# Multiply-adds of the modulation in chosen quanta, their sums turned later, two small steps of the attention on ScalarE

## The reference, cut to what matters

```python
for l in range(2):
    mod = silu(c) @ w_mod[l] + b_mod[l]          # 3 * 2048 columns: shift, scale, gate
    cmod = silu(c_ctx) @ w_mod[l] + b_mod[l]
    h = rmsnorm(x, norm_g[l]) * (1 + scale) + shift
    u = h @ w_in[l]                              # heads' q, k, v and the columns of ug
    y = concat(mixer_1(u), mixer_2(u)) * silu(ug)
    x = x + gate * (y @ w_o[l])
# layer 0: mixers a and b, layer 1: mixers c and d. One head of b: softmax(q k^T + mask, sink) v.
# One head of a: (softmax(q1 k1^T) - lam * softmax(q2 k2^T)) v, then its own rmsnorm.
```

## Time and profile before

| what | value |
|---|---|
| three timed runs | 2482.7 (median), 2484.22, 2478.44 us |
| the profiled execution | 2480.8 us |
| its span, first to last instruction | 2479.0 us |
| TensorE matmuls, busy | 2384.4 us, 96% |
| TensorE weight loads, busy | 1917.5 us, 77% |
| VectorE busy | 1526.8 us, 62% |
| ScalarE busy | 1034.1 us, 42% |
| mean granted TensorE clock | 0.994 |

### The profile page before, as it was taken

How to read it: one execution, slowest core, us unless ns; L and a number is a source line. 1 busy time by engine, 2 the same in 40 slices (tenths; PEclk the granted TensorE clock), 3 DMA queues, 4 the chain that set the end, 5 groups by cost and what they waited for, 6 DMA issues and landing times. The chain is left out here.

```text
span 2479.0 us, 31391 instructions
## 1 busy us (share of the span) xinstructions
PE 2384.4 (96%) x11660; PEld 1917.5 (77%) x11660; DVE 1526.8 (62%) x2575; ACT 1034.1 (42%) x1712; POOL 233.1 (9%) x329
## 2 busy tenths in 40 slices
PE   6999999999899999999899999999999999999998
PEld 1587778877668878887777788878878888898886
DVE  1368766777677777757646566676576544444654
ACT  3322333344443222433444445445454545654543
POOL 0001010011100000002121000001110001101100
PEclk8999999999999999999999999999999999999999
DMA  9957544444334565565464465756655576567653
GB/s 367 355 188 259 169 159 137 149 144 153 112 122 137 189 202 178 189 217 196 165 216 137 129 209 176 248 174 192 211 159 191 180 219 207 174 198 239 182 194 127
DMA packets 231174, 467.96 MB, mean 189 GB/s; under 512 B 17642, under 2 KB 42536, under 8 KB 229744
## 3 DMA queue, kind: packets, MB, share of 16 engines
q1 hardware_dynamic: 209104, 394.94, 49.2%
q0 software_dynamic: 21920, 71.01, 9.0%
HBM read 435.10 MB, written 30.79 MB: 188 GB/s over the span
## 5 line engine op out<-in xcount | busy, mean ns | idle before, releaser
L2112 PE MATMUL pp<-w_hi,hT_hi 128*128 128x512 f32 (+3 forms) x2904 | 1169.9, 403 | 9.1 <-DVE w_lo L1512 3.9
L2114 PE MATMUL pp<-w_hi,hT_lo 128*128 128x512 f32 (+3 forms) x2904 | 1115.8, 384 | 0.0
L2113 PE MATMUL pp<-w_lo,hT_hi 128*128 128x512 f32 (+3 forms) x2904 | 1113.4, 383 | 0.0
L1512 DVE TENSOR_TENSOR w_lo<-raw,w_hi 128x1024 fp32r<-128x1024 f32 (+4 forms) x568 | 669.4, 1183 | 572.2 <-ACT w_hi L1234 570.8
L1234 ACT ACTIVATE w_hi<-raw 128x1024 fp32r<-128x1024 f32 (+4 forms) x568 | 578.0, 1023 | 436.7 <-PE pp L2114 383.3
L2112 PEld LDWEIGHTS pp<-w_hi,hT_hi 128*128 128x128 f32 x2904 | 547.3, 188 | 137.4 <-issue 35.3
L2114 PEld LDWEIGHTS pp<-w_hi,hT_lo 128*128 128x128 f32 x2904 | 546.1, 188 | 105.7
L2113 PEld LDWEIGHTS pp<-w_lo,hT_hi 128*128 128x128 f32 x2904 | 548.0, 189 | 94.7 <-issue 6.9
L1612 DVE SCALAR_TENSOR_TENSOR arena<-raw,cT,arena 128x512 f32<-128x512 f32 x240 | 172.3, 745 | 0.7
L1612 DVE SCALAR_TENSOR_TENSOR xy<-raw,cT,xy 128x512 f32<-128x512 f32 x180 | 126.8, 744 | 0.0
L1393 ACT ACTIVATE arena<-pY 128x512 f32<-128x512 f32 (+2 forms) x114 | 62.1, 544 | 138.5 <-PE pY L2273 106.0
(11 more groups left out here) (311 smaller groups left out, 1764.5 us busy)
## 6 DMA issues: line engine op xcount, KB each, us to landing
raw<-in_w_in_dram SPq DMA_DIRECT2D x168, 512.0 KB, 4.1
raw<-in_w_mod_dram SPq DMA_DIRECT2D x158, 512.0 KB, 5.0
raw<-in_e_w_in_dram SPq DMA_DIRECT2D x102, 512.0 KB, 4.8
raw<-in_w_o_dram SPq DMA_DIRECT2D x64, 512.0 KB, 4.6
raw<-in_o_w_in_dram SPq DMA_DIRECT2D x64, 512.0 KB, 4.8
raw<-in_w_out_dram SPq DMA_DIRECT2D x64, 512.0 KB, 4.0
raw<-in_w_in_dram SPq DMA_DIRECT2D x56, 440.0 KB, 3.9
scratch_u<-ust POOLq DMA_DIRECT2D x35, 512.0 KB, 4.4
```

The lines of the kernel that those rows point to most:

```text
L1512: dve.tensor_tensor(w_lo[:, g.s % SPLIT, 0:n], raw_of(g)[:, 0:n], w_hi[:, g.s % SPLIT, 0:n].bitcast(F32), ALU.subtract).then_inc(lo_done, 1)
L2112: pe.matmul(dst, hT_hi[:, kk, o:o + P], hi[:, k, :], start=a, stop=False)
L2113: pe.matmul(dst, hT_hi[:, kk, o:o + P], lo[:, k, :], start=False, stop=False)
L2114: ins = pe.matmul(dst, hT_lo[:, kk, o:o + P], hi[:, k, :], start=False, stop=z)
```

## The change

Four things. (1) `Work.room` gives for each quantum how many multiply-adds it may hold, in place of the rates: 1 and 2 in turn up to quantum 164, 1 for twelve quanta, then 1 in each even quantum among the heads of b, three in eight among those of a (places 3, 4 and 7 counted from 308), 5 in four quanta from y0_3 to c_q0, and from there two in four. `LEAD` is 3. (2) Two more accumulators, of which one lies where mixer a's raw q and k were and waits for its last front, and the other in half of b_mask for the chunks gate1 that have one lane; the seven quanta between chunks are gone where the accumulator is another one. Load 0 of mixer c waits for the fold of shift1_3. (3) A fold comes at least four quanta after the last multiply-add. (4) The copies of mixer b (32) and the divisions `finish` of mixer a (32) are ScalarE's.

```diff
-LEAD = 4
+LEAD = 3
+    def room(self, slot):
+        b0, a0 = C["a_q0"].q0 + 4, C["a_q0"].q0 + 148
+        if slot < b0:
+            return 1 + slot % 2
+        if slot < b0 + 12:
+            return 1
+        if slot < a0:
+            return (slot - b0) % 4 in (0, 2)
+        if slot < C["y0_3"].q0:
+            return (slot - a0) % 8 in (3, 4, 7)
+        if slot < C["c_q0"].q0:
+            return 1 + (slot % 4 == 2)
+        return (slot - C["c_kv"].q1) % 4 in (0, 1)
...
-        rate = [(C["b_q1"].q0 + 4, 1.0), (C["b_kv"].q0, 1.4), (C["a_q0"].q0 + 14, 0.65), (C["y0_0"].q0 + 24, 0.55), (C["y0_3"].q0, 1.0), (C["c_q0"].q0, 0.5)]
-        free_b, taken_a = C["a_q0"].q0 + 152, C["y0_0"].q0 + 20
+        free_b, free_c, taken_a, taken_c = C["a_q0"].q0 + 152, C["y0_0"].q0 + 92, C["y0_0"].q0 + 20, C["c_q0"].q0 + 40
...
+            late = ch.name.startswith("gate1")
+            ch.lanes = (0,) if late else (0, 1)
+            if late:
+                slot, used = max(slot, self.sides[i - 1].macs_end + (9 if self.sides[i - 1].row is None else 1)), 0
+            elif i and slot + 4 > taken_a:
+                same = [p for p in self.sides[max(0, i - 2):i] if p.acc == (3 if i % 2 == 0 and slot > free_c else 2)]
+                if same and same[-1].macs_end + 9 > slot:
+                    slot, used = same[-1].macs_end + 9, 0
...
+                    while used >= self.room(slot):
+                        slot, used = slot + 1, 0
+                    used += 1
                     g.macs.append(slot)
...
-            first, second = [s for s in free if s >= ch.macs_end + 2][:2]
-            assert ch.acc < 2 or second < ch.macs_end + 7
+            first, second = [s for s in free if s >= ch.macs_end + 4][:2]
+            assert second < ch.macs_end + 8
...
-        accs = [xy[:, 0:2, 512:1024], xy[:, 2:4, 512:1024], b_mask]
+        accs = [xy[:, 0:2, 512:1024], xy[:, 2:4, 512:1024], b_mask, at(5632, 2, 512), at(8704, 1, 512)]
...
+                if m == "c" and n == 0:
+                    pool.wait_ge(*folded(C["shift1_3"]))
...
             def copy(m, n, u):
-                if m == "b":
+                copies(act_copy, act, m, n, u)
+
+            def finish(m, n, u):
+                if m != "a":
                     return
-                copies(act_copy, act, m, n, u)
+                x = plan.U[m, n, u]
+                act.wait_ge(probed, prob_n[x.key])
+                act.wait_ge(filled["O"], left["O", ("pv", *x.key)])
+                c0 = MIX["a"].ycol + 128 * n
+                act.activation(xy[:, x.qt, c0:c0 + 128], pO[:, 0:128], ACT.Copy, scale=rl[:, x.i % 4, 0:1]).then_inc(freed["O"], 1)
...
+                    elif ch.acc == 3:
+                        for key in (("front_q", "a", 7), ("front_k", "a", 7)):
+                            dve.wait_ge(filled[bank_of[key]], left[bank_of[key], key])
+                    elif ch.acc == 4:
+                        dve.wait_ge(*folded(C["shift1_3"]))
...
-            def copy(m, n, u):
-                if m == "b":
-                    copies(dve_copy, dve, m, n, u)
-
             def finish(m, n, u):
+                if m == "a":
+                    return
```

More of the change, by code:

```diff
@@ L185, in run @@
             self.put(ch, j)
-    def rate(self, table, slot):
-        return [r for s, r in table if s <= slot][-1]
+    def room(self, slot):
+        C = self.C
+        b0, a0 = C["a_q0"].q0 + 4, C["a_q0"].q0 + 148
[10 more added lines that the diff above has]
+        return (slot - C["c_kv"].q1) % 4 in (0, 1)
     def beside(self):
         C = self.C
-        rate = [(C["b_q1"].q0 + 4, 1.0), (C["b_kv"].q0, 1.4), (C["a_q0"].q0 + 14, 0.65), (C["y0_0"].q0 + 24, 0.55), (C["y0_3"].q0, 1.0), (C["c_q0"].q0, 0.5)]
-        free_b, taken_a = C["a_q0"].q0 + 152, C["y0_0"].q0 + 20
+        free_b, free_c, taken_a, taken_c = C["a_q0"].q0 + 152, C["y0_0"].q0 + 92, C["y0_0"].q0 + 20, C["c_q0"].q0 + 40
         self.macs = []
-        slot, credit = rate[0][0], 0.0
+        slot, used = C["b_q1"].q0 + 4, 0
         for i, ch in enumerate(self.sides):
-            lanes = (0,) if ch.name.startswith("gate1") else (0, 1)
-            ch.lanes = lanes
-            ch.mac0 = slot
+            late = ch.name.startswith("gate1")
[6 more added lines that the diff above has]
+                    slot, used = same[-1].macs_end + 9, 0
             for j in range(KT_ // GROUP):
@@ L205, in beside @@
                 self.sided.append(g)
[L206 to L209, removed]
+                for K, v in itertools.product(g.ks, ch.lanes):
+                    while used >= self.room(slot):
+                        slot, used = slot + 1, 0
+                    used += 1
                     g.macs.append(slot)
                     self.macs.append((slot, ch, K, v))
[L212 to L215, removed]
                 g.q0 = g.macs[0]
[L217 to L221, removed]
+            ch.mac0, ch.macs_end = ch.groups[0].macs[0], g.macs[-1]
+            if late:
+                ch.acc = 2 + 2 * (i % 2)
+            elif ch.macs_end + 9 < taken_a:
+                ch.acc = i % 2
+            elif i % 2 == 0 and ch.mac0 > free_c and ch.macs_end + 9 < taken_c:
+                ch.acc = 3
+            else:
+                ch.acc = 2
+                assert ch.mac0 > free_b
         n = 0
@@ L1491, in _ @@
             mine = {"evac": evac, "fold_row": fold_row, "sq_x": sq_x, "x_scale": x_scale, "sq": sq, "sq_x2": sq_x2, "x_turn": x_turn, "y_turn": y_turn, "lat_turn": lat_turn,
-                    "front_copy": front_copy, "exp": exp, "copy": copy, "squares": squares, "kpe_turn": kpe_turn,
+                    "front_copy": front_copy, "exp": exp, "copy": copy, "finish": finish, "squares": squares, "kpe_turn": kpe_turn,
                     "i_turn": i_turn, "ik_turn": ik_turn, "i_dots": i_dots, "g_soft": g_soft, "g_exp": g_exp,
@@ L2018, in _ @@
                     "lat_turn": lat_turn, "x2": x2, "n2_scale": n2_scale, "n3_half": n3_half, "x_gain": x_gain, "x_out": x_out, "front_copy": front_copy,
-                    "ssq": ssq, "rope": rope, "max": max_, "probs": probs, "copy": copy, "finish": finish, "a_scale": a_scale,
+                    "ssq": ssq, "rope": rope, "max": max_, "probs": probs, "finish": finish, "a_scale": a_scale,
                     "kpe_rope": kpe_rope, "kpe_turn": kpe_turn, "i_rope": i_rope, "ik_rope": ik_rope, "i_acc": i_acc_, "i_top": i_top,
```

## The result

The changed kernel takes 2486.95 us in the median of 8 runs (2483.42 to 2489.48), the kernel before 2481.45 beside it. The ratio is 1.0021, 95% interval 1.0012 to 1.0029: 5 us slower. 2476.9 was forecast, 6 us faster, with slower at 0.19: the median lies within the range that was given (2467 to 2489), but on the other side of the kernel before. The profiled execution took 2483.42 us, its span is 2481.4 (before: 2480.8 and 2479.0).

What follows compares the result with a forecast made beforehand. TensorE was taken to lead, busy 96%, with waits on other engines mostly in mixer a. Terms -10.8 - 1.5 + 0.5 + 2.0 + 4.0 = -5.8 us gave a median of 2476.9 from 2482.7; range 2467 to 2489.

Steps and rivals of the forecast that it cites:

- Mixer a, -10.8: Mixer a: 10.8 us gained from finishes on ScalarE, new places and later folds; bounds 6 and 16.1.
- 2.6 + 4.1 + 2.8: Heads of a, finishes on ScalarE: shorter probability waits 2.6, waits behind squares gone 4.1, sum-transpose waits gone 2.8 us.
- a gain of 1.3: Mixer a, places and folds: gains of 1.4, 0.5 and 0.6 us, less 1.2 for a fold pair that comes in.
- Copies of b, 0: Mixer b: its 32 copies moved to ScalarE gain nothing; value 0, bounds -1 us and +3.
- b_q1 and b_kv, +0.5: b_q1 and b_kv: rate up to 1.5 a quantum, VectorE 74% to 89%; costs 0.5 us, bounds 0 and 3.
- y0_3, +2.0: y0_3: 39 multiply-adds for 32, VectorE 83% to 91%, slightly late when y is turned; costs 2 us (0 to 5).
- Mixer c, -1.5: Mixer c: multiply-adds end at quantum 676 where they ended at 723; gain 1.5 us, bounds 0 and 3.
- out0, +4.0 (bounds 1 to 14): out0 chunks: rate 1.25, 150 multiply-adds for 107, VectorE 74% to 90%; costs 4.0 us, bounds 1 and 14.
- four prices of VectorE's own work: out0: chunk ends 2.1 us, a fold that comes 0.8, one that goes -0.8, two more multiply-adds into c 1.0.
- The 0.9: out0: weight loads held up by the reload of x, buffers with 5 quanta for 8; 0.9 us, between 0 and 4.1.
- The slower one: y0_3 to c: VectorE becomes the bound when late weights use up the slack; 17 us lost there, 2487.9, chance 19%.
- The mark that I had set for being wrong: Sign against the forecast: TensorE's idle time above 15 us between 775 and 1023 us, among three such signs.

Runs made afterwards that it cites:

- e1: Kernel before with only the copies of b and finishes of a moved to ScalarE; places, folds, accumulators and LEAD as before: ratio 0.9957.
- e2: Changed kernel with the copies of b and finishes of a back on VectorE; places, folds, accumulators and LEAD as changed: ratio 1.0050.
- e5: Changed kernel with all but the first multiply-add of six sums on 256 of 512 columns; instructions, order and loads stay: ratio 0.9977.
- e9: Changed kernel with LEAD 2 in place of 3: ratio 0.9965.
- e6: Changed kernel with 35 multiply-adds per 32 quanta of out0 for 40, none around the turn into c, c at quanta 2 and 3 of four: ratio 0.9957.
- e4: Changed kernel with mixer c's multiply-adds at quanta 2 and 3 of each four in place of 0 and 1: ratio 1.0015.
- e11: e6 with LEAD 2: ratio 0.9958 to the kernel before.
- e14: e12 with LEAD 2: ratio 0.9942 to the kernel before.
- e15: e14 without second multiply-adds in y0_3's last twelve quanta and out0_0's first four; three go to out0_3: ratio 0.9932.
- e12: e6 with folds two quanta apart from y0_3 on, and gate1's multiply-adds one a quantum in c_kv, none in c_q1: ratio 0.9941.
- e13: e1 with LEAD 2 in place of 4: ratio 0.9960 to the kernel before.

## Why the prediction was wrong, point by point

**Mixer a, -10.8: near in size, and that partly by luck.** The heads of a gave 12.7 us. The finishes on ScalarE were put at 9.5 (2.6 + 4.1 + 2.8) and give 6.7 (e1, profiled); waits behind the squares and behind finishes went as said, save one of 1.0, but the waits for the probabilities, which were to shrink by 2.6, stayed: 7.6 us in 12 waits for 7.3 in 10. Places and folds were put at a gain of 1.3 and give 6.0 in the heads alone (e2); a term too large and one too small made up for each other. The waits for L1912 in the changed kernel are at most 1.4 us where they were up to 1.8, and the new one behind a fold (1.2 us at quantum 363, 1.2 forecast) is as sized. Two others of 1.4 stand at quanta 387 and 419. The Trainium skill's rule of "ScalarE: Activation LUTs", section "Rules for kernel authors", to leave multiplications to VectorE, would have made this part worth nothing; e1 measures 10.7 us for the two moves, so here the place in the queue decided, not the price of the instruction.

**Copies of b, 0: right** (+0.3 in e1). What was not expected is that b's heads gain 3.0 us by the new places (e2; 85 multiply-adds there for 110), where I had written that no wait was there. The earlier trace rows show 4.7 us idle in that stretch, and I had put it at nothing. **b_q1 and b_kv, +0.5:** 0.0 with LEAD 3 at 87% of VectorE. **y0_3, +2.0:** +0.3. **Mixer c, -1.5:** +2.1; behind quantum 676, where no multiply-adds are left, d_kv gained 2.9 us, and c_kv and c_q1, which have about as many as before (24 for 22), lost 6.2.

**out0, +4.0 (bounds 1 to 14): the step that failed.** It measures +17.9, above the upper bound. I summed four prices of VectorE's own work at places that I knew and gave the weights 0.9, and wrote that "LEAD 3 in place of 4 only moves side loads back" and has no price of its own. By the runs:
- The order of side loads among the weights decides the sign of the whole. With the new places, LEAD 4, 3 and 2 give 1.0076, 1.0021 and 0.9965, and out0 costs 21.5, 17.9 and 10.9 us. At the old places no difference can be told. The step from 4 to 3, which I had put at nothing, was thus a gain of some 14 us, mostly in b, and one more step would have given 7.0 in out0. It was a price of the new places that LEAD sets, not an edit beside them.
- The estimate let a late weight delay the product that needs it. What it delays first is everything behind it in VectorE's queue. The weight that landed at 855 us was eight quanta early for its product, and TensorE waited 5.33 us at a fold, 4.61 of which stay when VectorE has half of its multiply-add work (e5). The 0.9 itself leaned on a misreading: the load in the earlier trace rows was issued at 873.57, after x had been read again (851 to 868), and took 6.3 us; the loads within that time took 11.2 and 13.4.
- The longest waits of out0 were paid again in clock. TensorE's idle time in out0 rose by 11.5 us (15.8 less 4.3), the stretch by 17.9. Of the other 6.4 us, an estimate of 5.1 is lost clock, by each window's length times what its mean clock lacks to 1.00: 3.4 from 852 to 868 us (mean clocks 0.93, 0.50 and 0.79) and 1.7 from 1017 to 1025 (0.78 and 0.79). What the rest is stays open. No row that I used had such a stretch, and no term stood for it.
- About 10 us of the 17.9 go with half of VectorE's multiply-add work (e5), 7.0 with LEAD 2 (e9). Fewer multiply-adds in out0 (122 for 151), which spare both, take away 15.8 (e6). No run halves the work and has LEAD 2 at once, so whether the two shares simply add isn't shown.

**The rivals.** The slower one had the right place and the right trigger, "weights which land later than needed" using up the slack, and 17 us for it, close to the 17.9 that out0 cost. That the sizes agree is luck: it counted 3 us at each of four chunk ends and 1 us at each of five fold pairs, and the ends waited 2.6 us in all, while one fold, the turn of x and the clock made the sum. I took its condition for unlikely because VectorE's shares stay near 90% and "a wait of TensorE gives VectorE the time back". The second is what failed: VectorE stood idle in the same wait (2.35 us in the timeline, 5.21 in e5), so it got nothing back. The mark that I had set for being wrong, idle time above 15 us from 775 to 1023, is met: 17.0 us in the same stages (757 to 1024), 15.8 of them in out0.

Open is why c's first keys wait 5.4 to 6.5 us in nearly all variants of the new places (7.9 in e4) and 3.1 to 3.8 at the old places, and 4.2 to 4.8 with LEAD 2 in e9, e11 and e14, but 6.1 in e15. In the changed kernel their stores and reloads run beside weight and side loads (1105 to 1127 us), but e12, which took the multiply-adds away from there, did not shorten it.

## What to carry to other kernels

When a helper's work shares an in-order queue with the preparation of weights, ask of each late transfer not when its product is due, but who stands behind it in the queue. Before raising a rate, test the lead of the loads that it brings: here one constant was worth more (14 us a step) than any part of the change. And give each wait of several microseconds a second price, for the clock after it: most of those above 3 us had it here.

## What the runs showed of the hardware

After TensorE had waited 5.33 us, the granted clock was at its lower level (0.50, 1.2 GHz) from 860 to 864 us, where matmuls of 128x512 follow every 0.43 us and not every 0.23, and back at 1.00 from 868. After the waits of 3.7 us (1017.86) and 2.5 us (1060.65) the next windows show 0.78 and 0.57; after those of 2.0 and 2.1 us (821.71, 938.89) it stayed at 1.00. The length of the wait alone doesn't decide, though. The same wait of 2.02 us at the gated product was followed by 0.58 in e4, one of 2.45 us in e11 by 1.00, and one of 3.75 us in e13 by 1.00; the clock was 1.00 ahead of all three. The windows right behind them, e4, e11, e13:

```profile
823.90:828.00 4.10, 4.02 (x13) 3.33 (x14) 4.10 (x6) 0.60 (x1) 0.00 (x0) 0.58 0.79 253
...
862.80:867.00 4.20, 4.20 (x21) 3.53 (x22) 3.47 (x6) 1.06 (x1) 0.00 (x0) 1.00 0.65 229
...
1114.20:1118.20 4.00, 3.92 (x21) 3.30 (x21) 3.72 (x6) 1.81 (x3) 0.00 (x0) 1.00 0.23 81
```

While x was read again, DMA was busy all the time (1.01, 407 GB/s), and weight loads took 12.7 us from issue to landing (842.53 to 855.23) where two issued just before (830.36 and 835.31) took 3.6 and 3.8. SP's loads issued in that stretch land in the order of issue, so the order decides which engine is held.
